# Two more weight buffers for the mixture of experts, expert 2 fixed in third place, and the last input product ahead of the next to last output product

## What is computed

```python
def _hier_moe(h, p):
    '''Top-1 expert group, then top-2 experts inside it; experts are SwiGLU MLPs.'''
    gl = (h @ p['w_group_router']).astype(jnp.float32)
    ...
    top_v, top_i = lax.top_k(el_sel, TOP_K)
    ...
    for gi in range(N_GROUPS):
        a = jnp.einsum('bsd,edf->bsef', h, p['w_e1'][gi])
        b = jnp.einsum('bsd,edf->bsef', h, p['w_e3'][gi])
        y = y + jnp.einsum('bsef,efd->bsd', jax.nn.silu(a) * b * w_all[:, :, gi, :, None], p['w_e2'][gi])
    return y
```

## Time and profile before

| | us |
|---|---|
| median of 3 runs | 1882.98 (1882.34 to 1887.23) |
| the profiled execution | 1894.46, of which its span is 1892.7 |
| TensorE busy | 1782.1, 94% of the span |
| transfers busy | 16 engines, mean 223 GB/s over the span |
| input products, 64-row part (L1319) | 126.9 and 118.0 busy |
| output products (L1340) | 76.2 and 54.9 busy |

### The profile page before, as it was taken

The page is one execution under the profiler, slowest core; times in us unless marked ns, Lnnn a source line. Parts: engine busy times, 40 slices in busy tenths (PEclk is TensorE's granted clock), DMA queues, the critical chain, the costliest instruction groups (busy, mean ns, idle before and its releaser), DMA issues.

```text
span 1892.7 us, 25310 instructions
## 1 busy us (share of the span) xinstructions
PE 1782.1 (94%) x10202; PEld 1095.7 (58%) x10202; DVE 813.7 (43%) x1850; ACT 442.7 (23%) x956; POOL 122.4 (6%) x160
## 2 busy tenths in 40 slices
PE   6999999999999989997789999999999998999887
PEld 3445656688777773332245565667888877333223
DVE  1295473565544451111133966536655455111113
ACT  3312344333100121010043134334321112111002
POOL 0001201000000030000020020010000003000002
PEclk9999999999999989998989999999999998999988
DMA  9662293413556658999952221323123335899994
GB/s 403 224 261 91 95 361 106 156 68 112 198 221 270 245 200 353 425 427 426 424 209 101 110 94 58 131 93 120 69 90 112 133 151 201 326 424 425 428 427 156
DMA packets 51926, 422.42 MB, mean 223 GB/s; under 512 B 6448, under 2 KB 7872, under 8 KB 28768
## 3 DMA queue, kind: packets, MB, share of 16 engines
q1 hardware_dynamic: 33696, 369.35, 48.9%
q0 software_dynamic: 9632, 33.07, 5.1%
q10 hardware_dynamic: 8480, 18.35, 2.6%
HBM read 386.38 MB, written 32.28 MB: 221 GB/s over the span
## 4 chain that ended last, share of the span: by engine, by line
PE 81%; DMA 14%; another core or an unknown queue 1%; issue 1%; DVE 1%; ACT 1%; SPq 0%; POOL 0%; ACTq 0%; DVEq 0%
PE psum L871 19%; PE psum L1148 19%; PE psum L1137 9%; PE psum L1319 8%; PE psum L874 7%; DMA pc<-we_in 6%; DMA ring<-we_in 6%; PE psum L1340 2%; PE psum L791 2%; PE psum L1324 2%; DMA ring<-wch_in 2%; PE psum L849 1%; PE psum L1223 1%; PE psum L1335 1%
## 5 line engine op out<-in xcount | busy, mean ns | idle before, releaser
L871 PE MATMUL psum<-hT,ring 128*128 128x384 f32 x1088 | 363.9, 489 | 0.1
L871 PEld LDWEIGHTS psum<-hT,ring 128*128 128x128 f32 x1088 | 202.9, 190 | 141.2 <-issue 12.4
L1137 PE MATMUL psum<-pc,ring 128*128 128x384 f32 x512 | 175.6, 486 | 0.0
L1319 PE MATMUL psum<-ring,scr 128*64 128x512 f32 x512 | 126.9, 653 | 30.9 <-DMA ring<-we_in 27.1
L2625 DVE TENSOR_TENSOR ytok<-pc,psum 128x256 f32<-128x256 f32 (+1 forms) x32 | 15.1, 471 | 323.1 <-ACT pc L1815 323.1
L1148 PE MATMUL psum<-hT,ring 128*128 128x192 f32 x768 | 143.0, 329 | 1.8 <-ACT vals L1514 1.8
L1148 PEld LDWEIGHTS psum<-hT,ring 128*128 128x128 f32 x768 | 126.1, 190 | 18.6 <-issue 9.6
L1319 PE MATMUL psum<-pc,scr 128*64 128x512 f32 x512 | 118.0, 615 | 18.7 <-DMA pc<-we_in 18.7
L2015 DVE SCALAR_TENSOR_TENSOR pc<-pc,par 128x384 f32<-128x384 f32 x240 | 127.2, 605 | 0.0
L874 PE MATMUL psum<-ring,hT 128*128 128x512 f32 x288 | 125.2, 593 | 0.0
L1137 PEld LDWEIGHTS psum<-pc,ring 128*128 128x128 f32 x512 | 94.4, 190 | 51.9
(11 more groups left out here) (421 smaller groups left out, 2383.8 us busy)
## 6 DMA issues: line engine op xcount, KB each, us to landing
ring<-we_in SPq DMA_DIRECT2D x48, 2048.0 KB, 17.8
pc<-we_in SPq DMA_DIRECT2D x48, 2048.0 KB, 20.0
ring<-wch_in SPq DMA_DIRECT2D x18, 2048.0 KB, 8.3
ring<-wgate_in SPq DMA_DIRECT2D x16, 2048.0 KB, 8.4
ring<-wmod_in SPq DMA_DIRECT2D x18, 1024.0 KB, 6.7
pc<-wmod_in SPq DMA_DIRECT2D x24, 768.0 KB, 7.7
ring<-wbr_in SPq DMA_DIRECT2D x16, 1024.0 KB, 4.8
ring<-wtok_in SPq DMA_DIRECT2D x6, 2048.0 KB, 8.9
```

Source lines behind the costliest of these rows:

```text
L871: mm = pe.matmul(F[:, 0:T], wv[:, k, n * P:(n + 1) * P], hT[:, k, :], start=k == 0, stop=k == KD - 1)
L1137: mm = pe.matmul(bank(7)[:, 0:T], wv[:, c, (n % 4) * P:(n % 4 + 1) * P], pc[:, MERGE_SLOT[i], c, :], start=c == 0, stop=c == 3)
L1319: mm = pe.matmul(bank(2)[BIG * h:BIG * h + BIG, :], x_h[:, k, 0:BIG], w[h][:, k, :], start=k == 0, stop=k == KD - 1, skip_group_check=True)
```

## The change

It has four parts.

1. **Two more rooms for input blocks.** Each is made of two pieces, 3072 and 1024 columns wide: `par` from `w_up` on with the tile `t_last_and_zeros`, and a new tile `late_room` with two thirds of `ytok`. The experts 2, 5, 8, 11 and 14 (`spare(e)`) have their input blocks there, the others in `ring` 0 and 1 or 3 and 4 by `e % 3`. Output blocks keep their two rooms. SP now issues the input blocks of expert e + 3 behind input product e. Eight blocks are issued ahead of the router. To make the place in SBUF, `t_last` and `zeros` become one tile and the scratch for GpSimd's transfers shrinks (`dynamic_dma_scratch_size=4096`).
2. **Expert 2 is fixed** in the third place, and so it is wide. `FREE` starts at 3, `RANK_AT` has 12 entries; the three wide free experts still stand at 4, 6 and 8.
3. **hidden(15) comes ahead of project(14)** on TensorE and VectorE, and ScalarE stores the rows of expert 14 behind its work for expert 15. The last blocks come in the order (15,0), (15,1), (13,2), (14,2), (15,2).
4. **The zeroing** is issued by ScalarE, ahead of the gate products, and no longer by GpSimd.

```diff
+def spare(e):
+    return e % 3 == 2
+SPARES = sum(spare(e) for e in range(NE))
+def expert_slot(e, j):
+    return 3 * (e % 2) + 2 if j == 2 else 3 * (e % 3) + j
...
-        plan += [(("exp", e, j), 3 * (e % 2) + j) for e in range(NE) for j in range(3)]
+        plan += [(("exp", e, j), expert_slot(e, j)) for e in range(NE) for j in range(3) if j == 2 or not spare(e)]
...
-FREE = range(2, NE - 1)
+FREE = range(3, NE - 1)
...
-RANK_AT = (3, 4, 0, 5, 1, 6, 2, 7, 8, 9, 10, 11, 12)
+RANK_AT = (3, 0, 4, 1, 5, 2, 6, 7, 8, 9, 10, 11)
...
+            def fill_spare(l, e):
+                for j, rooms in enumerate(spare_rooms):
+                    src, of = block_of(l, ("exp", e, j)), 0
+                    for room in rooms:
+                        width = room.shape[-1]
+                        sp.dma_start(room, src[:, of:of + width]).then_inc(rest_in.sem, 16)
+                        of += width
...
                 fill(l, ("exp", 1, 2))
+                expert.clear()
+                if l == 0:
+                    sp.wait_ge(rows_zeroed.sem, 32)
+                fill_spare(l, 2)
                 sp.wait_ge(slot_ready.sem, slot_ready.at(l, 2))
-                expert.clear()
                 for e in range(NE - 1):
...
-                    if e < NE - 2:
+                    if e + 3 < NE:
                         sp.wait_ge(xab_done.sem, xab_done.at(l, e + 1))
-                        fill(l, ("exp", e + 2, 0))
-                        if e < NE - 3:
-                            fill(l, ("exp", e + 2, 1))
+                        fill_inputs(l, e + 3)
                     if e >= 1:
                         sp.wait_ge(xy_done.sem, xy_done.at(l, parts_to(e)))
                         fill(l, ("exp", e + 1, 2))
-                    if e == NE - 3:
-                        fill(l, ("exp", NE - 1, 1))
...
+                hidden(NE - 1)
                 for n in range(2 if wide(NE - 2) else 1):
                     project(NE - 2, n)
-                hidden(NE - 1)
...
+                if l == 0:
+                    ac.wait_ge(setup_s.sem, 7)
+                    for rows_d in (xs_d, ys_d):
+                        ac.dma_start(rows_d.rearrange("(p s) (a n) -> p (s a) n", p=P, n=256),
+                                     zeros.rearrange("p (a n) -> p a n", a=1).to_broadcast([P, NE * CAP // P * 4, 256]))\
+                          .then_inc(rows_zeroed.sem, 16)
                 ac.wait_ge(fin_t.sem, fin_t.at(l, 2))
...
-                    if e == NE - 1:
-                        store_rows(e - 1)
                     ac.wait_ge(xab_done.sem, xab_done.at(l, e + 1))
...
-                    if 1 <= e < NE - 1:
+                    if e >= 1:
                         store_rows(e - 1)
...
+                open_hidden(NE - 1)
                 keep_out(NE - 2)
-                open_hidden(NE - 1)
```

More of the change, by code:

```diff
@@ L621, in fill, with fill_inputs @@
                 sp.dma_start(ring[slot], block_of(l, key)).then_inc(slot_in[slot].sem, 16)
+            def fill_spare(l, e):
[5 more added lines that the diff above has]
+                        of += width
+            def fill_inputs(l, e):
+                if spare(e):
+                    fill_spare(l, e)
+                else:
+                    fill(l, ("exp", e, 0))
+                    fill(l, ("exp", e, 1))
             def fill_half(n):
@@ L711, in _ @@
                 fill(l, ("exp", 1, 2))
+                expert.clear()
+                if l == 0:
+                    sp.wait_ge(rows_zeroed.sem, 32)
+                fill_spare(l, 2)
                 sp.wait_ge(slot_ready.sem, slot_ready.at(l, 2))
-                expert.clear()
                 for e in range(NE - 1):
-                    if e + 2 in FREE:
-                        p = e + 2 - FREE.start
-                        expert[e + 2] = sp.value_load(order_of[0:1, p:p + 1], min_val=FREE.start, max_val=FREE.stop - 1)
-                    if e < NE - 2:
+                    if e + 3 in FREE:
+                        p = e + 3 - FREE.start
+                        expert[e + 3] = sp.value_load(order_of[0:1, p:p + 1], min_val=FREE.start, max_val=FREE.stop - 1)
+                    if e + 3 < NE:
                         sp.wait_ge(xab_done.sem, xab_done.at(l, e + 1))
-                        fill(l, ("exp", e + 2, 0))
-                        if e < NE - 3:
-                            fill(l, ("exp", e + 2, 1))
+                        fill_inputs(l, e + 3)
                     if e >= 1:
@@ L1315, in hidden @@
                         pe.wait_ge(xg_ready.sem, xg_ready.at(l, e))
-                    w = [have(l, ("exp", e, j)) for j in range(2)]
+                    if spare(e):
+                        pe.wait_ge(rest_in.sem, 16 + 64 * (l * SPARES + e // 3 + 1))
+                        parts = [[r.rearrange("p (k n) -> p k n", n=512) for r in rooms] for rooms in spare_rooms]
+                        w = [[r[:, k, :] for r in rooms for k in range(r.shape[1])] for rooms in parts]
+                    else:
+                        w = [[have(l, ("exp", e, j))[:, k, :] for k in range(KD)] for j in range(2)]
                     for k in range(KD):
                         for h in range(2):
-                            mm = pe.matmul(bank(2)[BIG * h:BIG * h + BIG, :], x_h[:, k, 0:BIG], w[h][:, k, :],
+                            mm = pe.matmul(bank(2)[BIG * h:BIG * h + BIG, :], x_h[:, k, 0:BIG], w[h][k],
                                            start=k == 0, stop=k == KD - 1, skip_group_check=True)
@@ L1323, in hidden @@
                             part = slice(c % 2 * 256, c % 2 * 256 + 256)
-                            mm = pe.matmul(bank(3)[SUB * c:SUB * c + SUB, 0:256], x_h[:, k, BIG:CAP], w[c // 2][:, k, part],
+                            mm = pe.matmul(bank(3)[SUB * c:SUB * c + SUB, 0:256], x_h[:, k, BIG:CAP], w[c // 2][k][:, part],
                                            start=k == 0, stop=k == KD - 1, skip_group_check=True)
```

24 lines of the change are left out of this document (10 added, 14 removed).

## The result

The change takes 1915.6 us (four executions, 1914.7 to 1917.83) against 1883.4 for the kernel before, a ratio of 1.0169 with a 95% interval of 1.0151 to 1.0187: 31.8 us slower (28.4 to 35.2). The forecast was 1884.8, with 1868 to 1895 as its range. The likeliest of its slower rivals, ScalarE held by the zeroing, said 1905 and had a chance of 0.07.

A forecast was written before the change was run, and what follows sets the result against it. TensorE was busy 94% of the span, with the second half of each mixture waiting for weights. Layers +1.7 and +0.9, zeroing -0.7, gave +1.9 on 1882.98: 1884.9, put down as 1884.8, range 1868 to 1895.

The forecast's parts named there:

- ScalarE held by the zeroing: Rival, ahead of the gate products: the second zeroing issue holds ScalarE until room is there; +22, about 1905, chance 0.07.
- zeroing moved to ScalarE: Zeroing issued ahead of the gate products: 0.7 us gained at its old place, nothing lost at the new one.
- expert 2 wide: Third expert, after the router: its longer input product empties the queue for 0.9 us, bounds 0 and 3.6.
- two blocks fewer behind the router: Expert weights: eight blocks go ahead of the router, saving 2 x 5.39 = 10.8 us a layer, 21.6 in all.
- new end on top of it: End of the experts: store and gathers, hidden before, now follow project(14), with late-notice and clock terms added; +22.4.
- ScalarE's queue: Ahead of the gate products: two zeroing issues of 0.33 us fit ScalarE's free time, so no cost was taken.
- The rooms: Two more input rooms: two fewer blocks behind the router at 5.39 us each; (13,2) lands at 928.5 in layer 0.
- The end: After (13,2) lands: 18.4 us through project(14), then 22.1 to the stage's end; with added terms +1.7 and +0.9 by layer.
- the 1.5 for the clock: End of the experts: lower granted clock after project(13)'s wait lengthens the chain; 1.5 us taken, bounds 0 and 3.4.
- 0.8 for a late notice: End of the experts: the last output product, project(14), may be noticed late, 1.6 us or nothing; 0.8 taken.
- Part 4's gain: Zeroing taken from its old place under GpSimd: half of TensorE's 1.5 us idle there won back, 0.7.
- Fixed time for each piece: Rival, block loads in two pieces: twenty added transfers cost 3.1 us each, 62 us, about 1945; chance 0.02.

The follow-up runs named there:

- s1: The change with only the zeroing of the second row array issued later, behind the fifth pair of gate rows; 1.0057 and, on another chip, 1.0044 of before.
- z1: The kernel before with only the zeroing moved to ScalarE, as in the change; ratio 1.0137 to before, 25.8 us slower.
- s4: As s1, with before's end on all engines and last blocks ordered (13,2), (15,0), (14,2), (15,1), (15,2); ratio 0.9957 to before, 8.1 us faster.
- f1: The kernel before with expert 2 alone fixed in third place, and so wide; ratio 1.0022 to before, 4.1 us slower.
- s5: As s4, but from the fifth expert on the output block of expert e + 1 is issued ahead of expert e + 3's inputs; 0.9938 of before, 1869.4 us.

## Why the prediction was wrong, point by point

The account in us, by the forecast's own terms. "By medians" are differences of ratios, each uncertain by 2 to 5 and in part from different chips. "By traces" are differences of the time from the first input product to the end, both layers together, before as the mean of its three traces.

| term | forecast | by medians | by traces | from |
|---|---|---|---|---|
| zeroing moved to ScalarE | -0.7 (rival +22) | +21 (to +24); +25.8 alone | copy 23.7 later | the change less s1; z1 |
| expert 2 wide | +1.8 | +4.1 | -3.3 | f1 |
| two blocks fewer behind the router | -21.6 | -12 | -4 | s4 less f1 |
| new end on top of it | +22.4 | +19 | +14 | s1 less s4 |
| sum | +1.9 | +32 | | |

The two columns differ by up to 8 us in a term, so what stands clear of the noise is the hold, that the rooms gave far less than forecast, and that the new end costs well over ten us. The sign of expert 2's term is open.

**ScalarE's queue: the step that failed.** It said "two issues as SP's of 0.33 (same group) fit, two as GpSimd's, 4.6, would stand out by 2.7. I take nothing." It took the cost of an issue for that of issuing alone, and left out that the second could wait for the first. The row taken was of a transfer of 128 long pieces, the transfers to be priced had 6144 short ones, one behind another. What the runs showed in its place is a hold of 25.90 us (26.22 with this move alone), 22.00 us of idle TensorE, half clock behind them, and 21 to 26 us in the time. The only row of such transfers was GpSimd's, which returned after 2.3 us. That an issue on another engine's queue returns as fast wasn't in the trace. The rival had the mechanism, its place (the second issue returning later than 366.87) and nearly its price. That 22 meets the 22.00 of idle time so closely is luck: it took the first landing after GpSimd's 24.0 us, and here the first landed after 31.2 while ScalarE was let go 4.5 us ahead of that; and the half clock behind the wait wasn't in it. Its 0.07 was too small a chance for an issue whose cost no row bounded from above. The sentence cited from the Trainium skill ("DMA: Bandwidth & Descriptors", "Issuing engines are not separate DMA queues"), that the choice of engine only changes the sequencer's time, is literally kept: it is ScalarE's sequencer that lost the time. But the Trainium skill, in the same section, calls that time usually small relative to the transfer, and here the issue took 25.90 of the 48.1 us from its start to the landing. Where they differ, the measurement decides.

**The rooms: the term that was mis-sized.** The last output block came nearly when the forecast had it. In the change (13,2), the 38th block, lands at 953.73; the experts had started 23.4 us later than before, so the forecast's 928.5 stands for 951.9, and it was 1.8 late (1.6 in layer 1, 1852.93). Wrong was that the blocks fewer are worth 5.4 us each as soon as the rooms are there. They are worth that if the last wait is for the last blocks and all before them are served by need. The new order of issue put two inputs ahead of each output block, so output products waited (24.7 + 10.5 us in the change), and the old end with new rooms ended on (12,2). With the blocks by need the rooms give 11.7 + 4.1 by the medians, about 16 of the 21.6.

**The end.** The mechanism was right: chain from (13,2) to the end of project(14) 968.29 + 3.65 - 953.73 = 18.2 (18.4 forecast); from there 21.75 to the stage's end (22.1); in layer 1 the two are 18.2 and 23.0. The two added terms came out at nothing in layer 0. project(13) took 3.65 at full clock, so the 1.5 for the clock wasn't paid, and project(14) was followed at 971.88 by the next turn, so no 0.8 for a late notice. Between the first two traces the experts grew by 0.7 and 1.0 us, against +1.7 and +0.9 forecast, so from these alone the forecast of the experts looks right. By medians 8 to 11 us are left beside the hold, and not 1.9. By the medians' column the rooms gave 9.6 less than forecast, expert 2 cost 2.3 more, and the end 3.4 less, 8.5 in all; part of it may be noise. A side remark of the forecast, that the end is 9.3 to 13.4 us longer behind the last block, doesn't follow from its rows, which give 40.5 - 32.1 = 8.4 and 40.5 - 25.9 = 14.6. Nothing in the sum used it.

**Part 4's gain.** s1 starts the gates' first copy at 365.66 and s4 at 366.92, before's three traces at 366.0 to 367.0. A gain of 0.7 can't be told from none.

**Fixed time for each piece.** Refuted at its price of 62 us: s5 has all twenty added transfers and is below before. The forecast's estimate of 40 us took the 2.0 us of the Trainium skill, which the section states for transfers on GpSimd's path, for transfers of SP. s5 shows no such 40 us either.

**Range and chances.** The slower side held 0.21, of which 0.07 was the case that came. The range ended at 1895. (The sum itself is 1884.9; 1884.8 was put down.) The rival's own 1905 was 10 us short as well, by the 8 to 11 us of the rooms, the end and expert 2.

## What to carry to other kernels

An issue costs what the queue ahead of it costs: before a transfer of thousands of short pieces goes onto a computing engine's queue, ask what is ahead of it there and what that engine does next, and don't put another behind it until it has landed. If no row bounds such an issue, give the bad case real weight. More buffers shorten a transfer-bound stage fully only if the transfers stay in the order of need; when a lookahead is deepened, check what the extra loads now stand in front of. Work that leaves through DRAM and comes back (here store and gathers, 22 us) wants to start ahead of the last long product, not behind it.

## What the runs showed of the hardware

A second transfer of short pieces (1 KB) on ScalarE's queue held the engine until only 960 to 1222 of the pieces ahead were left, in nine held issues of three kernels: 25.90, 26.22 and, with transfers of 1536 pieces, 11.60 us and then 4.0 to 5.9 each. A single one of 6144 pieces returned in 0.72, and in 0.58 when it was issued 43 us after the one ahead had landed (400.2). GpSimd had taken both in 2.24 + 2.33. On SP's queue three blocks of 2 MiB, in 128 pieces of 16 KB each, were issued within 1.3 us from 643.10 on, before; so it isn't bytes that count there, and 384 pieces stay below the bound. Five transfers of 128 pieces from 703.30 on took 0.43 to 0.77 each in the change. Whether the bound is one of pieces on every queue, and what sets it, wasn't tried.

The time from the end of the dense work to the experts varied from 15.6 to 21.2 us between executions of the kernels here, with the same instructions on TensorE. In before's second trace, with 20.1 us, the granted clock in the stretch just ahead of the experts was 0.67:

```profile
694.00:704.00 10.00, 8.55 (x48) 8.41 (x48) 8.02 (x43) 0.00 (x0) 4.70 (x5) 0.67 0.40 155
```

In s1, with 15.7 us, the same ten us had full clock:

```profile
694.00:704.00 10.00, 8.91 (x61) 5.90 (x62) 6.72 (x36) 0.81 (x1) 5.79 (x6) 1.00 1.02 420
```

Before's third trace, with 15.6 us, has 1.00 there too, its first, with 19.3, has 0.66, and s1's second, with 17.1, has 0.83. So the stretch is the longer the lower its clock is. What decides the clock wasn't found.
